# Query and key projections as seven half products, with three rotating weight slots

## The chip, the cores and the metric

The kernel runs on one core of one Trainium2 chip. The metric is the device time of one launch in microseconds (us). Engines are named as in the profile: PE (TensorE) multiplies matrices, PEld is its weight load, DVE (VectorE) and ACT (ScalarE) do elementwise work and empty PSUM, POOL is GpSimd, SP issues nearly all loads from HBM.

## The reference, cut to what matters

One inference step of a two-layer trunk on 384 tokens (128 context tokens and 256 latent tokens), width 1024, all in float32. Layer 0 is differential attention, layer 1 retention; each is followed by a mixture of 16 experts. What the change touches are the projections of queries and keys:

```python
def diff_attention(h, w_qkv, ...):
    qkv = h @ w_qkv
    q = qkv[..., :DA_QK_WIDTH].reshape(B, N, DA_HEADS, 2, DA_HEAD_DIM)        # 8 heads of 128 columns
    k = qkv[..., DA_QK_WIDTH:2 * DA_QK_WIDTH].reshape(B, N, DA_HEADS, 2, DA_HEAD_DIM)
    ...
        q = axial_rope(q)
        keys = jnp.concatenate([cached[0], axial_rope(k)], axis=1)
    ...
def retention(h, w_qkv, ...):
    kd = RET_HEADS * RET_DK                                                    # 4 heads of 256 columns
    qkv = h @ w_qkv
    q = qkv[..., :kd].reshape(B, N, RET_HEADS, RET_DK)
    k = qkv[..., kd:2 * kd].reshape(B, N, RET_HEADS, RET_DK) * (RET_DK ** -0.5)
```

Besides these the first layers' modulation `silu(cond) @ w_ada[i] + b_ada[i]` matters, because its 24 weight pieces of 2 MB ("ada" units) are streamed during attention.

## The kernel before, in words

Activations lie feature-major: `hT` holds the normalised input as 8 tiles of 128 features by 384 tokens. Each engine has its own instruction stream, written out in program order, and the streams wait for each other on semaphores.

**PSUM.** `plan_jobs` numbers every accumulation. Job n uses bank n mod 8; `open_job` makes PE wait until job n-8 is emptied by ACT or DVE. `filled` and `emptied` are the two waits.

**Weights.** `ring` has six slots of 2 MB. `plan_units` lists all weight units in the order in which SP loads them, each with its slot and with the job after whose end the slot may be loaded anew. SP is one queue in that order: in `load` it waits for the slot's former user and issues (L569); whatever stands behind it waits too. During attention slots 0 to 3 rotate over the values' weights and the ada units, slot 4 holds the queries' weights of four heads and slot 5 the keys'. The second halves of these, units ("q", 1) and ("k", 1), follow when head 3 is done.

**Attention.** Steps s = 0 to 7, one for each head. In PE's stream a step is: transposed weights of head s-2 (`turn_a`), scores of head s-1, transposes, then queries of head s (`project("q", s)`, L771), output of head s-2 (`attend`, L873 to L876), keys of head s (L771), the rotary partner of the queries (`partner`, L833), in steps 0 and 4 the values (L808), an ada product (L673), the head norm's sum (L882), the keys' partner, an ada transpose (L680) and a second ada product. DVE does softmax maxima, weights, rotary products and norms. After step 7 a tail does the last four ada products between the last heads' work, and then comes the output projection (L937).

**Retention.** For each of four heads: queries and keys (`to_features`, 4 jobs of 8 matmuls on 384 columns), then values and two gates by seven products each (`seven_products`: one full product for token tile 0, seven of 4 matmuls on 256 columns for tiles 1 and 2 together; Winograd's form of Strassen's scheme, L786). Their operand sums are made by DVE (`weight_sums`, and `hS` once), and their results joined by DVE (`join`). Then come transposes, scores, states and outputs. Slots 0 to 3 rotate over retention's weights, slot 4 holds `hS` and the partial sums, slot 5 the weight sums.

Of the kernel before, what the change touches and what calls it, by code (L numbers as in the profile page):

```python
# [16 lines left out]
P = 128  # L17
D = 1024
KT = D // P
NP_TOK, NS_TOK = 128, 256  # L20
TOK = NP_TOK + NS_TOK
TT = TOK // P
# [31 lines left out]
RSLOT = 4  # L54
# [67 lines left out]
def plan_jobs():  # L122
# [24 lines left out]
    for s in range(HEADS):  # L147
# [24 lines left out]
    seven = lambda unit, who: [(unit + (0,), who), (unit + (1,), "act")] + [(unit + (i,), "dve") for i in range(2, 8)]  # L172
# [18 lines left out]
def plan_units():  # L191

    units = [(("ada", 0, u), ("ada", 0, u), u) for u in range(4)]
    qkv = lambda kind, g: ((kind, g), (kind, g, TT - 1) if kind == "v" else (kind, HALF * g + HALF - 1))
# [6 lines left out]
    for i, u in enumerate(turning):  # L201
# [4 lines left out]
        units.append(u + (i % 4,))  # L206
    assert len(turning) % 4 == 2
    order = ((2, 3, 0, 1, 4, 5), (4, 5, 2, 3, 0, 1))
# [15 lines left out]
    for h in range(RH):  # L224
        rest += [(("rqk", h), ("rk", h, 1)), (("rv", h), ("rv", h, 7)), (("rg", h, 0), ("rg", h, 0, 7)),
                 (("rg", h, 1), ("rg", h, 1, 7)), (("state", h), ("ro", h, TT - 1, 1))]
# [3 lines left out]
    units += [(("sums", i), ("rg", RH - 1, 1, 7), 4 + i) for i in range(2)]  # L230
# [4 lines left out]
def trunk_kernel(nc, ins, outs, scratch):  # L235
# [31 lines left out]
    with ctx:  # L267
# [81 lines left out]
        oT = sq  # L349

# [34 lines left out]
        m1, u2, u3, u5 = (sums[:, 2048 + 256 * i:2304 + 256 * i] for i in range(4))  # L385
        wT_ = ring[:, 5, :].rearrange("p (n k u) -> p n k u", n=4, k=4)
# [74 lines left out]
        hS_ready, wT_ready, joined = (sem(n) for n in ("hS_ready", "wT_ready", "joined"))  # L461
# [51 lines left out]
        def slot(name):  # L513
            return ring[:, slot_of[name], :]

# [8 lines left out]
        def _(sp):  # L524
# [46 lines left out]
            for name, _, _ in UNITS:  # L571
                if name[0] == "sums":
                    continue
                if name[0] != "moe":
# [6 lines left out]
                    if name == ("rv", 0):  # L581
# [54 lines left out]
        def _(pe):  # L636
# [137 lines left out]
            def seven_products(unit, n):  # L774
# [3 lines left out]
                to_tokens(unit + (0,), w, 0)  # L778
# [25 lines left out]
            def to_tokens(name, w, t):  # L804

                b = open_job(name)
                for kt in range(KT):
                    last = mm(b, hT[:, kt, P * t:P * t + P], w[:, kt, :], start=kt == 0, stop=kt == KT - 1)  # L808
                done(last)
# [9 lines left out]
            def project(kind, h):  # L819

                g, i = h // HALF, h % HALF
                if i == 0:
                    unit_wait(pe, (kind, g))
# [1382 lines left out]
```

## Time and profile before

| | |
|---|---|
| runs | 1444.04 us median of 3 (1442.41 to 1446.9) |
| the profiled execution | 1440.93 us, of which 1439.0 us are its span |
| PE matmuls busy | 1354.5 us (94%) |
| DVE, ACT, POOL busy | 517.8, 282.2, 47.2 us |
| HBM traffic | 344.83 MB, mean 240 GB/s |
| mean granted TensorE clock | 0.983 |

The profile page shows PE busy nearly throughout. In its row of 40 slices the DMA share is high in the first quarter (attention), at nine tenths or more through the experts, and low in retention. Each float32 matmul of the program stands as two instructions in the trace, so 256 query and key matmuls are the 512 of L771. A group in a timeline covers its instructions from the first's start to the last's end; ends of PE instructions are modelled and overlap the next, so the pitch of a group is (length minus the duration of one) over (count minus one), or the distance between starts of successive groups.

### The profile page before, as it was taken

How to read it: one execution, taken by the hardware profiler on the slowest of the kernel's cores; microseconds unless marked ns; L12 is line 12 of the kernel's file. 1: busy time of each engine (PE TensorE's matmuls, PEld its weight loads, DVE VectorE, ACT ScalarE, POOL GpSimd, SP SyncE). 2: the span in 40 equal slices, each digit the busy share in tenths (PEclk: the TensorE clock that was granted, in tenths of full speed). 3: DMA queues.
4: the chain of work that ended last, by engine and by line, in shares of the span. 5: the costliest groups of instructions: out<-in, count | busy, mean ns of one | idle time of the engine just before them, and what ended most of it. 6: DMA issues, size and time to landing. Idle time of an engine off the chain costs nothing.

```text
span 1439.0 us, 17852 instructions
## 1 busy us (share of the span) xinstructions
PE 1354.5 (94%) x6816; PEld 768.3 (53%) x6816; DVE 517.8 (36%) x1376; ACT 282.2 (20%) x580; POOL 47.2 (3%) x63
## 2 busy tenths in 40 slices
PE   5899999997998999889999999999998998899997
PEld 2456556555444444447667567576565544444434
DVE  3145355625111111554464653744513311111123
ACT  3143344411010111231120221212111100001013
POOL 1001200000000000100000000100100000000010
PEclk9999999998999999999999999999999899999998
DMA  9967686926999999912323423224534799579891
GB/s 363 322 244 231 224 279 237 380 95 238 392 396 350 398 395 378 388 64 94 117 82 117 146 88 110 95 89 139 182 118 174 254 398 387 190 258 398 324 399 52
DMA packets 162742, 344.83 MB, mean 240 GB/s; under 512 B 5929, under 2 KB 23554, under 8 KB 162626
## 3 DMA queue, kind: packets, MB, share of 16 engines
q1 hardware_dynamic: 150320, 319.19, 60.4%
q10 hardware_dynamic: 9362, 14.37, 2.7%
q0 software_dynamic: 2944, 9.65, 2.5%
q8 instruction: 82, 1.34, 0.4%
q14 instruction: 34, 0.28, 0.1%
HBM read 324.96 MB, written 18.22 MB: 238 GB/s over the span
## 4 chain that ended last, share of the span: by engine, by line
PE 85%; DMA 6%; DVE 4%; ACT 2%; SPq 2%; issue 1%; DVEq 0%; ACTq 0%
PE psum L1089 14%; PE psum L771 11%; PE psum L786 10%; PE psum L808 9%; PE psum L1120 7%; PE psum L986 7%; PE psum L1206 5%; PE psum L937 3%; PE psum L1198 3%; DMA ring<-in_moe_w_up 3%; PE psum L673 2%; PE psum L1031 2%; DMA ring<-in_da_w_qkv 2%; SPq L569 1%; PE psum L1060 1%
## 5 line engine op out<-in xcount | busy, mean ns | idle before, releaser
L771 PE MATMUL psum<-hT,ring 128*128 128x384 f32 x512 | 173.5, 498 | 8.8 <-DMA ring<-in_da_w_qkv 5.9
L1089 PE MATMUL psum<-ring,work 128*64 128x512 f32 x384 | 170.1, 593 | 2.6 <-DMA ring<-in_moe_w_up 2.6
L1090 PE MATMUL psum<-ring,work 128*64 128x512 f32 x384 | 170.2, 594 | 0.0
L771 PEld LDWEIGHTS psum<-hT,ring 128*128 128x128 f32 x512 | 99.0, 195 | 77.4 <-issue 8.3
L808 PE MATMUL psum<-ring,hT 128*128 128x512 f32 x288 | 125.9, 593 | 0.0
L986 PE MATMUL psum<-work 128*128 128x128 f32 x768 | 106.4, 292 | 5.5 <-issue 3.5
L1089 PEld LDWEIGHTS psum<-ring,work 128*64 128x64 f32 x384 | 51.8, 137 | 111.2 <-issue 111.0
L986 PEld LDWEIGHTS psum<-work 128*128 128x128 f32 x768 | 95.0, 200 | 28.2 <-issue 24.0
L1120 PE MATMUL psum<-ring,work 128*64 128x512 f32 x192 | 89.9, 612 | 1.3 <-issue 1.2
L1975 DVE COPY work<-psum 128x512 f32<-128x512 f32 x32 | 22.1, 692 | 191.2 <-PE psum L1121 191.2
L1121 PE MATMUL psum<-ring,work 128*64 128x512 f32 x192 | 90.0, 613 | 0.0
L1969 DVE TENSOR_TENSOR work<-work,psum 64x512 f32<-64x512 f32 x32 | 22.1, 690 | 187.1 <-ACT work L1463 187.0
L808 PEld LDWEIGHTS psum<-ring,hT 128*128 128x128 f32 x288 | 54.8, 190 | 63.7 <-issue 62.1
L786 PE MATMUL psum<-ring 128*128 128x256 f32 x384 | 86.8, 379 | 0.0
L1463 ACT ACTIVATE work<-psum 64x512 f32<-64x512 f32 x32 | 18.8, 588 | 314.8 <-PE psum L1090 314.8
L786 PEld LDWEIGHTS psum<-ring 128*128 128x128 f32 x384 | 73.1, 190 | 9.8
L786 PE MATMUL psum<-ring,hT 128*128 128x256 f32 x288 | 66.1, 379 | 0.0
L2003 DVE TENSOR_TENSOR ring<-ring 128x1024 f32<-128x1024 f32 x48 | 60.8, 1283 | 2.5 <-DVE work L2012 1.3
L786 PEld LDWEIGHTS psum<-ring,hT 128*128 128x128 f32 x288 | 54.8, 190 | 12.5 <-issue 5.7
L1640 DVE SCALAR_TENSOR_TENSOR xT<-psum,mod,xT 128x128 f32<-128x128 f32 x70 | 24.7, 412 | 94.7 <-PE psum L1206 62.1
L1090 PEld LDWEIGHTS psum<-ring,work 128*64 128x64 f32 x384 | 51.9, 137 | 0.0
L1120 PEld LDWEIGHTS psum<-ring,work 128*64 128x64 f32 x192 | 24.9, 140 | 47.2 <-issue 45.0
(338 smaller groups left out, 1810.0 us busy)
## 6 DMA issues: line engine op xcount, KB each, us to landing
ring<-in_w_ada SPq DMA_DIRECT2D x24, 2048.0 KB, 12.4
ring<-in_moe_w_gate SPq DMA_DIRECT2D x24, 2048.0 KB, 13.0
ring<-in_moe_w_up SPq DMA_DIRECT2D x24, 2048.0 KB, 17.4
ring<-in_moe_w_down SPq DMA_DIRECT2D x24, 2048.0 KB, 17.9
ring<-in_da_w_qkv SPq DMA_DIRECT2D x6, 2048.0 KB, 14.8
sq<-in_moe_w_gate SPq DMA_DIRECT2D x8, 1536.0 KB, 12.3
hT<-in_moe_w_up SPq DMA_DIRECT2D x8, 1536.0 KB, 15.0
work<-in_moe_w_down SPq DMA_DIRECT2D x24, 512.0 KB, 11.3
```

The costliest lines, as they stand in the source:

```text
L771: last = mm(b[:, 0:TOK], w[:, kt, col:col + P], hT[:, kt, :], start=kt == 0, stop=kt == KT - 1)
L786: last = mm(b[:, 0:256], rows[k], weights[k], start=k == 0, stop=k == 3)
L808: last = mm(b, hT[:, kt, P * t:P * t + P], w[:, kt, :], start=kt == 0, stop=kt == KT - 1)
L937: last = mm(b[:, 0:TOK], w[:, h, P * (ft % 4):P * (ft % 4) + P], oT[:, h, :], start=h == 0, stop=h == HEADS - 1)
L986: last = mm(out, htok[:, t, P * kt:P * kt + P], sel[:, t].rearrange("p x s -> p (x s)"), start=t == 0, stop=t == TT - 1)
L1089: mm(psum[0:BLK, x, :], xk, wg[kt], start=kt == 0, stop=kt == KT - 1)
L1090: last = mm(psum[BLK:P, x, :], xk, wu[kt], start=kt == 0, stop=kt == KT - 1)
L1120: mm(psum[0:BLK, 5 + x, :], eaT[:, x, k, :], wd[k][:, 0:512], start=k == 0, stop=k == 3)
L1121: last = mm(psum[BLK:P, 5 + x, :], eaT[:, x, k, :], wd[k][:, 512:D], start=k == 0, stop=k == 3)
L1198: last = mm(b, a, v, start=n == 0, stop=n == len(terms) - 1)
L1206: last = mm(b[:, 0:TOK], w[:, k, P * (ft % 2):P * (ft % 2) + P], roT(k), start=k == rows[0], stop=k == rows[-1])
L2003: V.tensor_tensor(wT_[:, part], x, y, ALU.subtract).then_inc(wT_ready, 1)
```

## The change

A head's queries and keys in attention become one product with the weights as two row halves (queries, keys), the features as two halves (K), and the tokens as two halves of 192. It is computed by seven products of 4 matmuls on 192 columns instead of two jobs of 8 on 384. Retention's queries get the same (their two feature tiles are the two halves), and its keys too. Sums of operands are made by DVE in place or in freed slots; ACT keeps product 1; DVE adds up the others. In retention the values now stand before queries and keys. Slot 3 holds `hA` and partial sums during attention, slot 0 holds `fS` during retention, so three slots rotate (`RSLOT = 3`).

```diff
-RSLOT = 4
+RSLOT = 3
+QK_ORDER = (1, 2, 4, 5, 6, 3, 7)
@@ plan_jobs, attention step s
-        jobs.append((("q", s), "act"))
+        jobs += [(("qk", s, 1), "act")] + [(("qk", s, i), "dve") for i in QK_ORDER[1:]]
         if s >= 2:
             jobs.append((("o", s - 2), "dve"))
-        jobs += [(("k", s), "act"), (("qswap", s), "dve")]
+        jobs.append((("qswap", s), "dve"))
@@ plan_jobs, retention head h
-        jobs += [(("rq", h, t), "act") for t in range(2)] + [(("rk", h, t), "act") for t in range(2)]
-        jobs += seven(("rv", h), "dve") + seven(("rg", h, 0), "act") + seven(("rg", h, 1), "act")
+        jobs += seven(("rv", h), "dve") + seven(("rq", h), None) + seven(("rk", h), None)
+        jobs += seven(("rg", h, 0), "act") + seven(("rg", h, 1), "act")
@@ plan_units
-    qkv = lambda kind, g: ((kind, g), (kind, g, TT - 1) if kind == "v" else (kind, HALF * g + HALF - 1))
+    qkv = lambda kind, g: ((kind, g), (kind, g, TT - 1) if kind == "v" else ("qk", HALF * g + HALF - 1, 7))
...
-        units.append(u + (i % 4,))
+        units.append(u + (i % 3,))
...
-    order = ((2, 3, 0, 1, 4, 5), (4, 5, 2, 3, 0, 1))
+    units.append((("sums", "a"), ("qk", HEADS - 1, 7), 3))
+    order = ((3, 1, 2, 0, 4, 5), (4, 5, 0, 3, 1, 2))
@@ SP: the retention tables move behind one more unit
-                    if name == ("rv", 0):
+                    if name == ("rg", 0, 0):
@@ PE, attention
+            def project(h):
+                a11, a12, a21, a22 = qk_blocks(h)
+                if h % HALF == 0:
+                    unit_wait(pe, ("q", h // HALF))
+                    unit_wait(pe, ("k", h // HALF))
...
+                product(1, a11, hT[:, 0:4, 0:192])
+                product(2, a12, h21)
+                if h == 0:
+                    pe.wait_ge(hA_ready, 4)
+                pe.wait_ge(qkS_ready, 4 * h + 2)
+                product(4, a21, hA[:, 2])
+                product(5, qkS1, hA[:, 0])
+                product(6, a22, hA[:, 3])
+                pe.wait_ge(qkS_ready, 4 * h + 4)
+                product(3, a11, hA[:, 1])
+                product(7, a12, h22)
...
             def partner(kind, h):
-                emptied(pe, (kind, h))
+                emptied(pe, ("qk", h, 7))
@@ DVE, attention
+            def low_sums(h):
...
+                V.tensor_tensor(qkS1, a21, a22, ALU.add).then_inc(qkS_ready, 1)
+                V.tensor_tensor(a21, a11, a21, ALU.subtract).then_inc(qkS_ready, 1)
+                dve.wait_ge(qkS_ready, 4 * h + 1)
+                filled(dve, ("qk", h, 1))
+                V.tensor_tensor(a11, qkS1, a11, ALU.subtract).then_inc(qkS_ready, 1)
+                dve.wait_ge(qkS_ready, 4 * h + 3)
+                filled(dve, ("qk", h, 2))
+                V.tensor_tensor(a12, a12, a11, ALU.subtract).then_inc(qkS_ready, 1)
+            def join_qk(h):
...
+                add(raw[:, 0, 0:192], 2, am1).then_inc(evac["dve"], 1)
+                link(add(au2, 3, am1))
+                link(add(au3, 4, au2))
+                dve.sem_inc(evac["dve"], 1)
+                link(add(au5, 5, au2))
+                add(raw[:, 1, 192:TOK], 5, au3).then_inc(evac["dve"], 1)
+                add(raw[:, 1, 0:192], 6, au3).then_inc(evac["dve"], 1)
+                add(raw[:, 0, 192:TOK], 7, au5).then_inc(evac["dve"], 2)
...
                     ada([ADA_UNITS[2 * s - 1]])
+                low_sums(s)
+                if s:
                     weights_of(s - 1)
+                join_qk(s)
@@ PE, retention (seven_features has the same seven products, on 192 columns)
                 seven_products(("rv", h), 3 * h)
+                unit_wait(pe, ("rqk", h))
+                seven_features("rq", h)
+                seven_features("rk", h)
@@ DVE, retention
+                join(("rv", h), rv)
+                feature_sums("rk", h)
+                join_features("rq", h, rq)
+                rotate(0, rq)
+                weight_sums(("rg", h, 0), range(4))
+                join_features("rk", h, rk)
+                rotate(1, rk)
...
                     if h + 1 < RH:
-                        weight_sums(("rv", h + 1), ((0,), (1,), (2, 3))[t])
+                        if t < 2:
+                            weight_sums(("rv", h + 1), ((0, 1), (2, 3))[t])
+                        else:
+                            feature_sums("rq", h + 1)
```

Before the loops DVE makes `hA` (attention, 4 differences of 768 columns) and `hF` (retention, 3 of 768 and 2 of 384).

PE's stream where step 3 ends and step 4 begins, before. L673 are ada products, L771 the queries, `slot_fullN` the wait for the weights in slot N:

```order
L673 MATMUL psum<-ring,cond 32x512 [waits act_evacuated,slot_full3]
...
L673 MATMUL psum<-ring,cond 32x512 [waits act_evacuated,slot_full0]
...
L771 MATMUL psum<-hT,ring 128x384 [waits act_evacuated,slot_full4]
...
L771 MATMUL psum<-hT,ring 128x384 [waits act_evacuated,slot_full5]
...
L808 MATMUL psum<-ring,hT 128x512 [waits act_evacuated,slot_full1]
...
L673 MATMUL psum<-ring,cond 32x512 [waits act_evacuated,slot_full2]
```

The same place after; L692 are the ada products, L882 the seven products, L858 the values:

```order
L692 MATMUL psum<-ring,cond 32x512 [waits dve_evacuated,slot_full1]
...
L692 MATMUL psum<-ring,cond 32x512 [waits dve_evacuated,slot_full2]
...
L882 MATMUL psum<-hT,ring 128x192 [waits act_evacuated,slot_full5,slot_full4]
...
L858 MATMUL psum<-ring,hT 128x512 [waits dve_evacuated,slot_full0]
...
L692 MATMUL psum<-ring,cond 32x512 [waits dve_evacuated,slot_full1]
```

The first product now waits for slots 4 and 5 together. Step 4's first ada unit lies in slot 1, which step 3's first ada product still reads; before, its slot 2 had been free since step 2. In SP's list this unit stands directly ahead of ("q", 1) and ("k", 1), before and after.

DVE's stream in a step after the change, from the softmax maxima (L1717) on. L1745 to L1752 are the sums of weights, L1726 begins the softmax weights, and the adds of the products (L1759) follow these:

```order
L1717 TENSOR_REDUCE work<-psum 128x1 [waits ps_filled] x6
L1647 TENSOR_REDUCE mod<-psum 128x8 [waits ps_filled]
L1650 TENSOR_TENSOR mod<-mod,cols0 128x8 [waits dve_evacuated]
L1745 TENSOR_TENSOR work<-ring 128x512
L1746 TENSOR_TENSOR ring<-ring 128x4x128
L1749 TENSOR_TENSOR ring<-work,ring 128x4x128 [waits ps_filled,qkS_ready]
L1752 TENSOR_TENSOR ring<-ring 128x4x128 [waits ps_filled,qkS_ready]
L1726 RECIPROCAL work<-work 128x2 [waits act_evacuated]
L1727 TENSOR_TENSOR work<-work,lam_s 128x1 [waits dve_chain]
```

Before, the reciprocal stood directly behind the two rows that read and write `mod`; four sums of 512 columns now stand between.

## Rows read from the trace of the kernel before

**Rows 1.** The page: DVE's busy tenths in 40 slices; groups with busy us, mean ns.

```profile
DVE  3145355625111111554464653744513311111123
...
L771 PE MATMUL psum<-hT,ring 128*128 128x384 f32 x512 | 173.5, 498 | 8.8 <-DMA ring<-in_da_w_qkv 5.9
...
L786 PE MATMUL psum<-ring 128*128 128x256 f32 x384 | 86.8, 379 | 0.0
...
L786 PEld LDWEIGHTS psum<-ring 128*128 128x128 f32 x384 | 73.1, 190 | 9.8
```

**Rows 2.** PE's timeline of attention step 5: start us, length us, what, count.

```profile
194.80 5.33 PE L771 MATMUL psum<-hT,ring 128*128 128x384 f32 x16
...
201.49 5.32 PE L771 MATMUL psum<-hT,ring 128*128 128x384 f32 x16
...
207.17 1.92 PE L673 MATMUL psum<-ring,cond 128*32 128x512 f32 x16
209.02 0.91 PE L882 MATMUL psum<-rdiag,ones 128*128 128x384 f32 x2
...
210.21 0.60 PE L680 MATMUL psum<-base_sb,ada_rows 128*128 128x128 f32 x4
...
217.02 5.33 PE L771 MATMUL psum<-hT,ring 128*128 128x384 f32 x16
```

**Rows 3.** PE's timeline in retention, heads 0 and 2.

```profile
618.26 22.34 PE L771 MATMUL psum<-hT,ring 128*128 128x384 f32 x64 [1.85 <-DVE hT L1625]
640.44 7.03 PE L808 MATMUL psum<-ring,hT 128*128 128x512 f32 x16
...
650.76 5.34 PE L786 MATMUL psum<-ring 128*128 128x256 f32 x24
...
815.25 20.80 PE L771 MATMUL psum<-hT,ring 128*128 128x384 f32 x64
```

**Rows 4.** SP's timeline of loads: start us, length of issuing, what, count.

```profile
135.12 7.05 SPq L569 DMA_DIRECT2D ring<-in_da_w_qkv  x2
...
244.60 7.04 SPq L569 DMA_DIRECT2D ring<-in_da_w_o  x2
253.60 3.93 SPq L569 DMA_DIRECT2D ring<-in_w_ada  x2
```

**Rows 5.** DMA issues of 136 to 143 us and 256 to 258 us: KB, us to landing.

```profile
ring<-in_da_w_qkv SPq DMA_DIRECT2D x1, 2048.0 KB, 7.7
...
ring<-in_w_ada SPq DMA_DIRECT2D x1, 2048.0 KB, 14.5
```

**Rows 6.** PE's timeline at the start; a bracket is idle time and its releaser.

```profile
36.61 7.12 PE L771 MATMUL psum<-hT,ring 128*128 128x384 f32 x16 [2.56 <-DMA ring<-in_da_w_qkv]
...
47.03 7.12 PE L771 MATMUL psum<-hT,ring 128*128 128x384 f32 x16 [3.30 <-DMA ring<-in_da_w_qkv]
...
54.42 20.76 PE L808 MATMUL psum<-ring,hT 128*128 128x512 f32 x48
```

**Rows 7.** Stretches after that idle time: PE, PEld, DVE, ACT, POOL, PEclk, DMA.

```profile
48.00:51.00 3.00, 3.00 (x6) 1.49 (x6) 0.00 (x0) 0.00 (x0) 0.00 (x0) 0.50 1.05 387
51.00:54.00 3.00, 3.00 (x11) 1.81 (x10) 0.00 (x0) 0.00 (x0) 0.00 (x0) 0.97 1.05 387
```

**Rows 8.** PE's timeline at attention's end.

```profile
268.26 1.92 PE L673 MATMUL psum<-ring,cond 128*32 128x512 f32 x16
...
271.74 1.92 PE L673 MATMUL psum<-ring,cond 128*32 128x512 f32 x16 [0.20 <-DMA ring<-in_w_ada]
...
276.05 4.68 PE L937 MATMUL psum<-sq,ring 128*128 128x384 f32 x14
```

**Rows 9.** DVE's timeline in retention: sums, the end of head 1, an add.

```profile
629.89 0.69 DVE L2040 TENSOR_TENSOR ring<-hT,ring 128x512 f32<-128x512 f32 x1
...
832.93 0.69 DVE L2110 TENSOR_TENSOR work<-work 128x512 f32<-128x512 f32 x1
...
851.93 0.42 DVE L2012 TENSOR_TENSOR work<-psum,ring 128x256 f32<-128x256 f32 x1
```

More of the change, by code:

```diff
@@ L229, in plan_units @@
     turn_in()
-    units += [(("sums", i), ("rg", RH - 1, 1, 7), 4 + i) for i in range(2)]
+    units += [(("sums", i), ("rg", RH - 1, 1, 7), s) for i, s in enumerate((4, 5, 0))]
     moe(1)
@@ L349, in trunk_kernel @@
         oT = sq
+        att_end = sum(ap.shape[1] for name, ap in wa.items() if name != "at")
+        qkS1 = work[:, att_end:att_end + 512].rearrange("p (k t) -> p k t", k=4)
+        hA = ring[:, 3, 0:3072].rearrange("p (n k t) -> p n k t", n=4, k=4)
+        am1, au2, au3, au5 = (ring[:, 3, 3072 + 192 * i:3264 + 192 * i] for i in range(4))
         wr_ = carve({"tab": ret_np.shape[1], "dist": (dist_np.shape[1] + 1) // 2, "q": 2 * TOK, "k": 2 * TOK,
@@ L514, in slot, with qk_blocks @@
             return ring[:, slot_of[name], :]
+        def qk_blocks(h):
+            at = P * (h % HALF)
+            views = [slot((kind, h // HALF)).rearrange("p (k n) -> p k n", k=KT)[:, :, at:at + P] for kind in "qk"]
+            return [w[:, 4 * k:4 * k + 4, :] for w in views for k in range(2)]
         def y_rows(i):
@@ L817, in _, with product @@
             swap = table(att_tab, att_at, "swap")
[L819 to L823, printed above, removed]
-                w = slot((kind, g)).rearrange("p (k n) -> p k n", k=KT)
-                to_features((kind, h), w, P * i, 0 if (kind, h) == ("q", 0) else None)
+            def project(h):
[3 more added lines that the diff above has]
+                    unit_wait(pe, ("k", h // HALF))
+                def product(i, weights, rows):
+                    b = open_job(("qk", h, i))
+                    for k in range(4):
+                        if h == 0 and i < 3:
+                            h_wait(pe, 0, k + 4 * (i - 1))
+                        last = mm(b[:, 0:192], weights[:, k, :], rows[:, k, :], start=k == 0, stop=k == 3)
+                    done(last)
+                h21, h22 = hT[:, 4:8, 0:192], hT[:, 4:8, 192:TOK]
+                product(1, a11, hT[:, 0:4, 0:192])
[9 more added lines that the diff above has]
+                product(7, a12, h22)
             def partner(kind, h):
-                emptied(pe, (kind, h))
+                emptied(pe, ("qk", h, 7))
                 if h == 0:
@@ L1140, in _ @@
             for h in range(RH):
-                unit_wait(pe, ("rqk", h))
-                w = slot(("rqk", h)).rearrange("p (k n) -> p k n", k=KT)
-                for t in range(2):
-                    to_features(("rq", h, t), w, P * t, 2 if h == 0 and t == 0 else None)
-                for t in range(2):
-                    to_features(("rk", h, t), w, RDK + P * t)
                 def turn_o(hh, tiles=range(TT)):
@@ L1500, in _, with keep_first @@
             for h in range(RH):
[L1501 to L1508 removed]
+                def keep_first(unit, n, width=256, scale=1.0):
+                    if n:
+                        act.wait_ge(joined, n)
+                    filled(act, unit + (1,))
+                    A(m1[:, 0:width], bank(unit + (1,))[:, 0:width], ACT.Copy, scale=scale).then_inc(evac["act"], 1)
+                keep_first(("rv", h), 5 * h)
+                keep_first(("rq", h), 5 * h + 1, 192)
+                keep_first(("rk", h), 5 * h + 2, 192, RDK ** -0.5)
                 dt_ = lambda n: table(dist_tab, dist_at, n)
@@ L1517, in _ @@
                     act.wait_ge(ro_ready, TT * h)
[L1519 to L1526 removed]
                 for d in range(2):
[L1528 removed]
+                    n = 5 * h + 3 + d
                     filled(act, ("rg", h, d, 0))
```

156 lines of the change are left out of this document (115 added, 41 removed).

## The prediction

> **What bounds the kernel now.** I read four views in this order. The page first: PE works nearly throughout, so the end is set by PE's program order, and a change is worth what it takes out of that order minus the gaps it opens. Then PE's timeline of an attention step [rows 2]: the step repeats every 22.22 us (194.80 to 217.02) and its groups follow each other without a bracket of idle time, so a step lasts as long as PE's instructions. Retention is the same [rows 3]. Then SP's timeline [rows 4], because the change takes one of four rotating slots away: how early a load may start matters now. Last the start and the end of attention [rows 6, 8], the only places of that stage where PE already waits for a load: 2.56 and 3.30 us for queries' and keys' weights, 0.20 us for the last ada unit. These two places have no slack.
>
> **The gain on PE.** 384 columns cost 0.3225 us an instruction (20.80 less 0.50, over 63 [rows 1, 3]), 256 columns 0.2157 (5.34 less 0.38, over 23 [rows 1, 3]). The difference is 0.107 us for 128 columns, so 192 columns should cost 0.2157 - 0.0534 = 0.1625 us. No row shows 192 columns. From below it is 0.16 (192 columns at that slope alone). From above it is 0.19, if the weight load, which is recorded with 190 ns [rows 1], no longer hid. The nearest row is the transposes, which load 128x128 weights for only 128 columns: 4 in 0.60 us, less about 0.27 for the last one, is 0.11 us each [rows 2]. A load thus fits behind 128 columns, and I take 0.1625. The Trainium skill, "TensorE: Matmul & The Clock Gate", section "Back-to-back issue gap", says otherwise: the simple per-column formula undercounts small matmuls, which it gives as about 81 ns against 56 at 128 columns, because the weight load shares the budget. The trace's transposes do not agree with that surcharge; by it, as an estimate, the 25 ns on each of 896 instructions would take 22 us back.
>
> - Attention, a head: 32 x 0.3225 = 10.32 us becomes 7 x 4 x 2 = 56 x 0.1625 = 9.10. Gain 1.22, eight heads 9.8 us.
> - Retention, a head: 64 x 0.3225 = 20.64 becomes 112 x 0.1625 = 18.20. Gain 2.44, four heads 9.8 us.
>
> Together 19.5 us.
>
> **Start of attention.** Before, head 0's queries ran from 36.61 while the keys' weights came, and the keys began at 47.03 [rows 6]. The first product now waits for both slots, so PE stands still until 47.03 (the loads ahead of it are unchanged). Each resumption after such a gap costs: 16 instructions took 7.12 instead of 5.33 us [rows 2, 6], with the granted clock at 0.50, the 1.2 GHz level, from 48 to 51 us and 0.97 after it [rows 7]. That is 1.8 us. Products end at 47.03 + 9.10 + 1.8 = 57.9. Then the rotary partner waits for the adds: product 3 comes sixth of seven, and six adds of 192 columns hang on it, at about 0.36 us each (256 columns take 0.42 [rows 9]), 2.2 us and 0.3 of handover, against 1.3 us of product 7. 1.2 us stay open. With the partner's 0.4 us the values begin at 59.6 instead of 54.42. Lost 5.2 us, so 6.4 against the gain already counted.
>
> **The other steps.** Step 1 has the same open 1.2 us. From step 2 on `attend` (about 1.5 us between queries and keys [rows 2]) stands there and covers it. The weight sums on DVE (4 of 512 columns, 0.69 each [rows 9]) stand ahead of the softmax weights, for which ACT's third pair of exponentials waits, and with it the banks that products 6 and 3 need. Counting that chain through, it is late by about 0.2 us a step and 0.4 in step 1. The other DVE work (some 5 us a head) lies in its idle half: the slices of attention show 1 to 6 tenths [rows 1]. Cost 1.6 + 6 x 0.2 = 2.8 us; bounds 0 and 9 us (1.3 us in each of seven steps, a whole product late).
>
> **Step 4, the lost slot.** Before, ("q", 1) was issued at 135.12, right behind head 3's queries, and ("k", 1) at about 141.8 [rows 4], landing 7.7 us later [rows 5], just ahead of step 4. Now the ada unit ahead of them in SP's list reuses the slot that step 3's first ada product reads. SP stands there until that product ends: 14.22 us into the step before (194.80 to 209.02 [rows 2]), 13.2 now (1.22 less, 0.2 more). Only then three units of 2 MB go out. The first lands after 7.7 us; each further one takes 5.4 to 6.0 (the second output unit, issued at about 251.3 [rows 4], and two ada units behind it had landed 14.5 us after 257.2 [rows 5], three units in 20.4 us with 2.3 of fixed delay). The keys' weights land 19.2 us after the issue, 32.4 into step 3. PE is there at 22.22 - 1.22 + 0.2 = 21.2. It waits 11.2 us and resumes slowly for another 1.8: 13.0 us.
>
> **The tail.** The same happens in step 7. Before, the two output units and then the last two ada units were issued between 244.6 and 257.2 [rows 4]. Now ("ada", 1, 9) needs the slot of step 7's first ada product, and both output units stand behind it in the queue. From the end of that product (before: step 7 began one step after step 6, 217.02 + 22.22 = 239.24, and 14.22 on is 253.5 [rows 2]) five units follow each other: the fourth lands after about 24 us, the fifth after 7.7 + 4 x 5.6 = 30. PE wanted them 14.8 and 18.3 us after that point (268.26 and 271.74 [rows 8]). Of the 11.7 us most is spent ahead of the fourth. With half a microsecond of slow clock 12.2 us. The experts' loads behind them are late by the same amount as PE, so nothing is given back.
>
> **Retention's seams.** Head 0: DVE finishes `hS` at 630.6 [rows 9]; product 3 of the values is wanted at 618.26 + 6.9 + 3.4 + about 1.5 of slow clock = 630.1, since the queries no longer stand ahead. With handover 0.6 us. Heads 1 to 3: DVE ends the previous head at 833.6 [rows 9], now about 834.1 with `feature_sums` in place of two weight sums, and must then empty the values' first bank (0.69), which the queries' first product wants at 815.25 + 18.95 = 834.2 [rows 3]. 0.5 us a head. Together 2.1 us, bounds 0 and 8. Retention's slots are loaded at least 30 us before use even with three, at no cost; if that cover went, each would show as a DMA wait. Moving the tables behind one more unit costs nothing, since values now come first.
>
> **Sum.** 19.5 gained; 6.4 + 2.8 + 13.0 + 12.2 + 2.1 = 36.5 lost: 17 us slower. Against the profiled execution's 1440.93 that is 1458; it ran 3.1 below the median of the runs, so I put 17 on 1444.04: 1461.
>
> **Rivals.**
> - *Both waits are hidden* (SP's loads arrive in time, by faster landing or because PE is later there than I count). For it: before, both places ran with almost no wait. Against it: the semaphore waits follow from the slots, and 2 MB at the 387 GB/s of [rows 7] is 5.4 us whatever the order. Then 25.2 us fall away: 8 faster, 1436.
> - *One of them is hidden*, or both are half as long: 1449.
> - *The weight load shows at 192 columns.* At 0.19 us, 896 x 0.0275 = 24.6 us more: 1486. Against it: the transposes' 0.11 us [rows 2]. The skill's page named above would have it so.
> - *DVE becomes late in every step* (adds or bank waits at their bounds, 6 us in attention and 6 in retention above my terms): 1473. For it: these seams are the tightest part of my count.
>
> **How the numbers follow.** My case 0.65 (1452 to 1470), both hidden 0.07, one hidden 0.12, weight load 0.04, DVE late 0.12. The range 1449 to 1473 leaves the extremes out. About 0.3%, 4.3 us, is what a measurement of this kernel can tell from no change: faster 0.07, same 0.04 (from the lower end of the one-hidden case), slower 0.89.
>
> **What would show it.** In the profile after: matmuls of 192 columns at 0.16 us pitch, 896 of them; a PE wait of about 11 us for a load of `in_da_w_qkv` in attention's middle, with a clock near one half right after it; waits for `in_w_ada` of 9 and 2 us at its end; PE's start of the values near 59.6; a plain step of 21.2 us. I am wrong if step 4 begins without a DMA wait, if a plain step is not shorter than 22.2, or if retention's head is not about 2 us shorter than before.

## The result, and the profile after

The changed kernel takes 1484.11 us (median of 4 runs, 1482.38 to 1486.42) against 1445.24 (4 runs): 1.028 times, 95% interval 1.0261 to 1.0299. The forecast was 1461, with a range from 1449 to 1473. The sign was right, and so were the four costs named in attention (its start, the other steps, step 4, the tail); the size was not. One of the prediction's own signs of being wrong came true: retention's heads did not become about 2 us shorter. The profiled execution took 1482.38 us, its span 1480.6, which is 41.6 more than the span before (forecast 17, so 24.6 are missing).

The page of the changed kernel. The second, third and fourth rows are busy tenths in 40 slices and PE's granted clock; the last is PE's new product line (busy us, mean ns, idle time):

```profile
span 1480.6 us, 18884 instructions
...
PE   5799699698989999889999999999999898889997
...
DVE  2348538624211111268386484683611411111123
...
PEclk9899899898989999989999999999999899999998
...
L882 PE MATMUL psum<-hT,ring 128*128 128x192 f32 x192 | 38.4, 355 | 23.4 <-issue 12.1
```

PE's timeline of attention: the start, step 4, a plain step (5 to 6), and the end (start us, length us, what, count, idle time ahead and its releaser).

```profile
46.66 5.46 PE L882 MATMUL psum<-hT,ring 128*128 128x192 f32 x16 [10.23 <-DMA ring<-in_da_w_qkv]
...
60.42 14.75 PE L858 MATMUL psum<-ring,hT 128*128 128x512 f32 x34
...
168.70 4.50 PE L882 MATMUL psum<-hT,ring 128*128 128x192 f32 x16 [12.11 <-issue]
...
212.29 2.77 PE L882 MATMUL psum<-hT,ring 128*128 128x192 f32 x16
...
233.56 2.77 PE L882 MATMUL psum<-hT,ring 128*128 128x192 f32 x16
...
294.08 3.64 PE L692 MATMUL psum<-ring,cond 128*32 128x512 f32 x16 [11.13 <-DMA ring<-in_w_ada]
...
303.81 4.68 PE L1007 MATMUL psum<-sq,ring 128*128 128x384 f32 x14
```

The values start at 60.42 us [rows 6: 54.42], the plain step lasts 21.27 [rows 2: 22.22], step 4 waits 12.11, the tail 11.13, and the output projection begins at 303.81 [rows 8: 276.05]. The pitch at 192 columns is (2.77 - 0.355) / 15 = 0.161 us. This is the picture that was forecast, but for the tail, where one wait of 11.13 stands in place of two of 9 and 2. PE's row at step 4 names no releaser ("issue"). DVE's first weight sum waits for the same two slots; it starts at the same 168.70 and is released by the load:

```profile
168.70 0.69 DVE L1745 TENSOR_TENSOR work<-ring 128x512 f32<-128x512 f32 x1 [11.76 <-DMA ring<-in_da_w_qkv]
```

The span as a ledger of stages, from the starts of PE's groups:

| stage | before | after | more | forecast |
|---|---|---|---|---|
| to the output projection | 276.05 | 303.81 | +27.8 | +24.7 |
| to the first expert's product | 71.89 | 72.56 | +0.7 | 0 |
| experts of layer 0 | 270.32 | 281.24 | **+10.9** | 0 |
| retention, to its output projection | 393.75 | 392.57 | **-1.2** | -7.7 |
| to layer 1's first expert | 114.40 | 115.26 | +0.9 | 0 |
| experts of layer 1, to the end | 312.59 | 315.16 | +2.6 | 0 |

Two rows hold 17.4 us of the miss. Retention's -1.2 compares two single traces. The changed kernel's retention code takes 392.4 to 394.8 us in five traces (after, experiments 4, 5, 6 and 9), before's code 393.7 to 395.4 in four (before, experiments 1, 2 and 10), so a gain of about 1 us is what can be said.

In the experts nothing had been changed but the order of their slots. There the distance between the first products of neighbouring experts is the thing to read. It is 13.91 us in both kernels (24.23 where an overflow block runs, a conditional piece of code for tokens beyond an expert's first 64). Before, it exceeds that by about one microsecond at the seventh (25.17), the tenth (15.02) and, by a weight load, the fifteenth expert. After, the third takes 19.14, the fourth 19.00 and the fourteenth 18.65, 15.1 us more together. Before's own excess is gone there: the seventh takes 24.23, the tenth 13.91 and the fifteenth 12.94 (before 14.85), which leaves about 11. PE's waits in that stage, before and after (us in total, times, longest):

```profile
PE psum L1103 <- DVE work L1969: 3.8, 2, 2.3
...
PE psum L1089 <- DMA ring<-in_moe_w_up: 1.7, 1, 1.7
...
PE psum L986 <- issue: 1.0, 1, 1.0
```

```profile
PE psum L1056 <- issue: 5.2, 2, 3.4
PE psum L1190 <- issue: 3.8, 2, 3.4
PE psum L1173 <- DVE work L2073: 3.8, 2, 2.3
```

The new ones end with "issue": nothing that the profile shows released them. PE's timeline at the third and fourth experts of the changed kernel:

```profile
411.21 1.38 PE L1056 MATMUL psum<-work 128*128 128x128 f32 x10
414.40 2.07 PE L1056 MATMUL psum<-work 128*128 128x128 f32 x8 [1.81 <-issue]
...
418.60 1.12 PE L1190 MATMUL psum<-work 128*64 128x512 f32 x1
...
421.66 0.59 PE L1190 MATMUL psum<-work 128*64 128x512 f32 x1
...
432.55 0.46 PE L1173 MATMUL psum<-base_sb,work 64*128 64x64 f32 x4
...
437.23 0.61 PE L1190 MATMUL psum<-ring,work 128*64 128x512 f32 x1 [3.35 <-issue]
```

The first gap stands inside one run of 18 equal matmuls, where the program has no wait of any kind, so it is not a late load and not another engine. Behind the gap the matmuls take 1.12 instead of 0.59 us, and the rows of those stretches (PE, PEld, DVE, ACT, POOL, granted clock, DMA) have the clock at 0.52, the 1.2 GHz level, for 7 us. So a gap of 1.8 us costs 5.2 here.

```profile
414.40:421.50 7.10, 7.10 (x26) 4.56 (x28) 0.00 (x0) 0.98 (x2) 0.00 (x0) 0.52 1.03 401
421.50:430.00 8.50, 8.50 (x42) 2.67 (x38) 0.95 (x2) 0.00 (x0) 0.00 (x0) 1.00 1.05 392
```

The second gap is ACT's: PE waits for the turned activations, and ACT's timeline shows it with nothing to wait for either.

```profile
430.46 0.59 ACT L1527 ACTIVATE work<-psum 64x512 f32<-64x512 f32 x1 [11.16 <-PE psum L1160]
436.74 0.38 ACT L1530 ACTIVATE work<-psum 128x256 f32<-128x256 f32 x1 [5.69 <-issue]
```

PE's transposes that L1530 reads (L1173) ended at 433.0, so ACT stood still for 3.7 us. What lies between ACT's two instructions is a branch over the overflow block (each expert has one, on PE, ACT and DVE). The DMA records show packets of code (queues of kind "instruction") near both gaps. The queues of the stretch 411.5 to 414.0 us, and of 434.0 to 436.5 (packets, MB, share of 16 engines):

```profile
q1 hardware_dynamic: 468, 0.95, 102.1%
q8 instruction: 1, 0.02, 2.8%
```

```profile
q1 hardware_dynamic: 280, 1.02, 102.6%
q14 instruction: 1, 0.01, 0.8%
```

Packets are 16 KB in q8 and 8 KB in q14 (the page has 85 packets and 1.39 MB, 37 and 0.30), beside weight loads that fill the DMA engines. That q8 is PE's queue and q14 ACT's is inferred from these places; the profile doesn't name a queue's engine. The q14 packet stands inside ACT's gap (435.00 to 435.25, the gap 433.0 to 436.7). The q8 packet stands at 411.75 to 412.00, just ahead of PE's gap (412.59 to 414.40). A packet is no proof of a wait: layer 0's experts have 27 of q8 in either kernel, and the aligned kernel of experiment 9 has one at the same place of the third expert (7.6 us behind its first product) without a gap.

The theory from here on, called *code*: after some branches an engine waits for its own instructions, which ones depends on where the branch stands in its stretch of code, and the change shifted that by altering the length of PE's and ACT's programs. The Trainium skill, "Runtime: NRT & Kernel Launch", section "Instruction fetch mechanics", has the rule: code comes in blocks of 16 KiB, and a taken branch beyond what is held forces a fetch; the size of q8's packets agrees, while the 8 KB ones of q14 are not in the rule. The rival, called *loads*: the changed order of the experts' slots and the late start of their loads.

Retention, head 1 of the changed kernel, PE's timeline:

```profile
755.28 7.03 PE L858 MATMUL psum<-ring,hT 128*128 128x512 f32 x16
...
765.61 5.34 PE L805 MATMUL psum<-ring 128*128 128x256 f32 x24
772.86 1.97 PE L805 MATMUL psum<-ring,hT 128*128 128x256 f32 x8 [1.91 <-ACT work L1608]
774.66 1.89 PE L805 MATMUL psum<-ring 128*128 128x256 f32 x8
777.57 2.84 PE L834 MATMUL psum<-hT,ring 128*128 128x192 f32 x16 [1.02 <-DVE work L2120]
```

Two gaps where before [rows 3] had none. L1608 is ACT's head norm, which empties the bank of product 6; L2120 is DVE's copy of the first value tile, which empties the bank of the queries' first product. DVE's timeline ahead of them:

```profile
761.18 3.43 DVE L2107 TENSOR_TENSOR ring<-ring 128x1024 f32<-128x1024 f32 x2
...
771.80 0.69 DVE L2142 TENSOR_TENSOR ring<-ring 128x512 f32<-128x512 f32 x1
...
773.01 1.76 DVE L2145 TENSOR_TENSOR ring<-ring 128x512 f32<-128x512 f32 x1
774.80 0.69 DVE L2147 TENSOR_TENSOR ring<-ring 128x512 f32<-128x512 f32 x1
...
776.74 0.68 DVE L2120 COPY work<-psum 128x512 f32<-128x512 f32 x1
```

Two value sums (3.43 us, where one of 1.23 stood before) come ahead of the last tile's statistics, for which ACT waits; four query sums (3.7 us) come ahead of the copy. Heads 1 to 3 take 99.35, 97.67 and 97.88 us, before 98.4 each.

### The profile page after: what moved, and what is told of

It is laid out like the page before. It is cut to its first block, busy times and chain, and to the rows that moved or that the text cites. A ratio compares the mean times of both kernels' runs of the same rounds, so it can differ in the third digit from the quotient of the medians.

```text
span 1480.6 us, 18884 instructions
## 1 busy us (share of the span) xinstructions
PE 1351.4 (91%) x7200; PEld 826.6 (56%) x7200; DVE 599.7 (41%) x1561; ACT 271.6 (18%) x564; POOL 47.4 (3%) x63
## 3 DMA queue, kind: packets, MB, share of 16 engines
q8 instruction: 85, 1.39, 0.4%
## 4 chain that ended last, share of the span: by engine, by line
PE 77%; DVE 9%; DMA 6%; issue 3%; ACT 3%; SPq 2%; DVEq 0%; ACTq 0%
PE psum L1159 15%; PE psum L1190 8%; PE psum L805 7%; PE psum L858 7%; PE psum L1056 7%; PE psum L882 5%; PE psum L834 5%; PE psum L1272 5%; PE psum L1007 3%; DMA ring<-in_da_w_qkv 2%; PE psum L692 2%; PE psum L1101 2%; DMA out_new_ret_fwd<-work 2%; DMA ring<-in_w_ada 1%; SPq L588 1%
## 5 line engine op out<-in xcount | busy, mean ns | idle before, releaser
L858 PE MATMUL psum<-ring,hT 128*128 128x512 f32 x288 | 128.9, 604 | 1.9 <-DVE hT L1682 1.9
L858 PEld LDWEIGHTS psum<-ring,hT 128*128 128x128 f32 x288 | 55.6, 194 | 68.8 <-issue 68.5
L1697 DVE SCALAR_TENSOR_TENSOR xT<-psum,mod,xT 128x128 f32<-128x128 f32 x70 | 24.7, 412 | 94.6 <-PE psum L1272 62.1
L692 PE MATMUL psum<-ring,cond 128*32 128x512 f32 x384 | 49.1, 633 | 15.0 <-DMA ring<-in_w_ada 14.9
L882 PE MATMUL psum<-hT,ring 128*128 128x192 f32 x192 | 38.4, 355 | 23.4 <-issue 12.1
## 6 DMA issues: line engine op xcount, KB each, us to landing
work<-in_moe_w_down SPq DMA_DIRECT2D x24, 512.0 KB, 11.6
```

The costliest lines, as they stand in the source:

```text
L692: last = mm(b[32 * j:32 * j + 32, :], cond[:, kt, :], w[:, kt, :], start=kt < 4, stop=kt >= 4)
L882: last = mm(b[:, 0:192], weights[:, k, :], rows[:, k, :], start=k == 0, stop=k == 3)
```

## Experiments

A ratio is against the kernel before, run beside the experiment, with its 95% interval. An experiment of one run is read by its trace and not by its time.

**1. The slot alone.** The kernel before, with three rotating slots in attention.

```diff
-        units.append(u + (i % 4,))
-    order = ((2, 3, 0, 1, 4, 5), (4, 5, 2, 3, 0, 1))
+        units.append(u + (i % 3,))
+    order = ((3, 1, 2, 0, 4, 5), (4, 5, 3, 1, 2, 0))
```

> The kernel before with only the slot given up: three rotating slots in attention, and the experts' loads in the changed kernel's order of slots; all products as before, so every engine's code is that of before. Theory code (the experts' extra 11 us in the changed kernel are waits of PE and ACT for their own code, after the branch that each expert has): the code is the same, so the stage from the first expert's product to retention's first stays at 270.3 us, within 2. Theory loads (they come from the changed order of the experts' slots and from loads that start late): it grows to about 281 us. Both: step 4's queries wait some 11 us and cost 13 with the clock, the last two ada products wait 11 to 12, so that the output projection starts some 25 us later than before's 276.05, and the time is about 1466 us by the first theory, 1477 by the second.

1467.26 us, ratio 1.0182 (1.0152 to 1.0212). The output projection starts at 298.85, 22.8 later than before; the experts of layer 0 take 267.7 us, 2.6 less than before (expected was no change, within 2).

```profile
157.98 1.65 PE L771 MATMUL psum<-hT,ring 128*128 128x384 f32 x2 [6.58 <-DMA ring<-in_da_w_qkv]
```

```profile
287.56 3.22 PE L673 MATMUL psum<-ring,cond 128*32 128x512 f32 x16 [10.19 <-DMA ring<-in_w_ada]
...
294.54 1.92 PE L673 MATMUL psum<-ring,cond 128*32 128x512 f32 x16 [2.41 <-DMA ring<-in_w_ada]
```

The slot is worth 23 us by itself, at the two places forecast. Step 4 waits only 6.6 here (expected 11), since the queries run while the keys' weights come. The order of layer 0's slots is the changed kernel's, the stage starts 23 us late (there 28), and no time is lost in the experts: against *loads*.

**2. Attention's part alone**, retention as before with four slots (the diff's parts on `qk`, `low_sums`, `join_qk`, `project` and the three slots).

> Attention's seven half products and its three slots, retention as before with four slots. Both theories: output projection starts at 303.8 us as in the changed kernel, retention takes 394 us as before. Theory code: PE's code ahead of the experts is that of the changed kernel, so the experts of layer 0 lose the same 11 us (waits at the third, fourth and fourteenth expert), those of layer 1 something else, since the code between differs: 1480 us within 5. Theory loads: experts of layer 0 also 281 us. The two differ only in layer 1, where code gives a new pattern.

1478.25 us, ratio 1.0243 (1.0216 to 1.027). Output projection at 305.57. Layer 0's third, fourth and fourteenth experts take 19.13, 19.12 and 20.07 us; layer 1 loses less (302.3 us from its first product to PE's last instruction, after 306.9). As *code* has it, though it doesn't separate the theories in layer 0.

**3. Retention's part alone**, attention as before with four slots (the parts on `seven_features`, `feature_sums`, `join_features`, and three slots in retention).

> Attention as before with four slots, retention's queries and keys by seven half products, three slots there. Output projection at 276.05 us and experts of layer 0 at 270.3 us by both theories (code ahead of them is before's). Retention from its first product to the rows of its output projection: 392.6 us as in the changed kernel, 1.2 less than before. Theory seams (two new waits of 0.9 and 1.0 us per head from the second on take what the product saves): those waits are there again. Rival (the saving is lost only because the stage starts late in the changed kernel): the waits are gone and the stage takes 388 us. Time 1440 us by the first, 1435 by the second, and up to 5 more or less by what layer 1's experts wait for their code.

1445.82 us, ratio 1.0028 (1.0013 to 1.0043): not faster. Retention takes 394.9 us, where the first two kernels, with before's code, take 395.3 and before's own profile 393.8. Both waits are there (4.8 for ACT and 3.1 for the copy over three heads), so it is the stage's own order that eats the gain, not its late start. Layer 0's experts: 270.6 us, before's pattern. In layer 1, whose code is shifted, the second expert takes 19.00.

**4. Filler on PE.** The changed kernel with idle increments.

```diff
+            for _ in range(128):
+                pe.sem_inc(filler, 1)
```

> The changed kernel with 128 increments of a semaphore that nobody waits for, put on PE ahead of the first query product, where PE idles for 10 us. Theory code: the branches and the ends of the code's blocks stand elsewhere against each other, so the excess over 13.91 us (24.23 with an overflow block) moves to other experts; the stage's length changes by several us, up or down. Theory loads: the same experts (third, fourth, fourteenth) lose the same 5.2, 5.1 and 4.7 us, and the stage takes 281.2 us again.

1484.98 us (one run). The third and fourteenth experts are clean (13.94 and 13.91). The fourth keeps its loss (20.22: ACT's, whose code is untouched), and the tenth now takes 17.60, the thirteenth 15.06. The stage's sum stayed (280.97), where several us up or down were expected. The places moved, as only *code* has it. The filler wasn't free: step 0 begins 7.1 us later.

**5. Step 4's weights first.**

```diff
-        if u[0] == ("ada",) + ADA_UNITS[9]:
+        if u[0] == ("ada",) + ADA_UNITS[8]:
             units += [qkv("q", 1) + (4,), qkv("k", 1) + (5,)]
```

> The changed kernel with the loads of step 4's queries and keys put one place earlier in the one queue of loads, ahead of the ada unit that waits for a product of step 3. If step 4's wait of 12.1 us comes from the lost slot through that order: the loads are issued some 4 us earlier and have no 5.4 us load ahead of them, so the wait falls to about 3 us, the slow clock behind it (1.8 us) goes, and the output projection starts at about 293 us instead of 303.8. If the wait is bound by the slots of the queries themselves, it stays above 8 us. The experts' waits for code stand at the third, fourth and fourteenth expert as in the changed kernel, since PE's code is the same.

1476.18 us (one run). The wait falls from 12.11 to 2.74, and the output projection starts at 293.47, both as expected. The second is in part luck: the slow clock, which was to go, stayed (16 products took 4.50 us even behind a gap of 2.7), and 1.4 us were won at the start of attention instead, in the same code. The third expert has the gap of the changed kernel, but the clock stayed high behind it:

```profile
404.13 1.16 PE L1056 MATMUL psum<-work 128*128 128x128 f32 x8 [1.80 <-issue]
```

The granted clock of 403.5 to 411 us is 1.00, and the expert takes 15.97 instead of 19.14.

**6. The tail's slots.** Slots 3 and 4 for the last two ada units, ahead of the output projection's (the order of the experts' slots changes with them).

```diff
+        if u[0] == ("ada",) + ADA_UNITS[18]:
+            units.append((("sums", "a"), ("qk", HEADS - 1, 7), 3))
+        units.append(u + ((3, 4)[i - 20] if i >= 20 else i % 3,))
+    units += [(("wo", n), ("wo", 4 * n + 3), (5, 0)[n]) for n in range(2)]
```

> The changed kernel with the last two ada units in slots 3 and 4, which the last queries and keys leave free, and loaded ahead of the output projection's two units, which go to slots 5 and 0. If the tail's wait of 11.1 us is the order of loads and slots: it falls under 2 us and the output projection starts at about 291.5 us instead of 303.8. If the tail is bound by the transfers as such (six loads of 5.4 us one behind another), the start moves by under 4 us. Experts as in the changed kernel.

1468.51 us (one run). The wait falls from 11.13 to 2.64 and the output projection starts at 295.19, 8.6 earlier (forecast 12; the wait was to fall under 2). Most of the tail's loss was order; that the remaining 2.64 us are the transfers' was not tested.

**7. Sums early**, in retention's head norm.

```diff
-                            weight_sums(("rv", h + 1), ((0, 1), (2, 3))[t])
+                            weight_sums(("rv", h + 1), ((0, 1, 2), (3,))[t])
```

> The changed kernel with the next head's four value sums on DVE split as three and one over the first two tiles of the head norm instead of two and two. If the wait for ACT (2.6 us over three heads) comes from the two sums (3.4 us) ahead of the last tile's norm: it goes, since three sums (3.7 us) fit the first tile's gap behind the state's stores, and the second tile has one (1.2 us). The other wait (DVE's copy of the first value tile, 3.1 us) falls too, as DVE is 2.2 us earlier there. Retention's stage 392.6 us becomes 388 to 390. Rival (ACT is late by the stores of the state, not by DVE): no change.

1480.61 us (one run). The waits in heads 1 to 3, after and here:

```profile
PE psum L834 <- DVE work L2120: 3.1, 3, 1.0
PE psum L805 <- ACT work L1608: 2.6, 3, 1.9
```

```profile
PE psum L834 <- DVE work L2120: 3.1, 3, 1.0
PE psum L805 <- ACT work L1608: 1.4, 1, 1.4
```

Half a hit: the stage takes 391.5 us, not 388 to 390. Heads 2 and 3 lose ACT's wait and take 97.47, but head 1 keeps 1.4 us of it. The copy's wait did not move, but DVE did not come earlier either: its query sums begin at 771.78 us here and at 771.80 in the changed kernel, 0.2 to 0.5 us earlier in each head instead of 2.2, since what the shorter list saves goes into DVE's own waits for ACT (0.38 us idle and 1.30 instead of 0.68 for the product behind them). So this run doesn't say whether an earlier DVE would help the copy; experiment 11 moves the sums themselves.

**8. All repairs.** 5 to 7 together (slots adapted), and the values ahead of the queries and keys at steps 0 and 4, so that their weights land beside the value products; at step 4 DVE's sums go behind the softmax weights.

```diff
-    units += [qkv("q", 0) + (4,), qkv("k", 0) + (5,)]
-    turning = [qkv("v", 0)]
+    units += [qkv("v", 0) + (4,), qkv("q", 0) + (5,), qkv("k", 0) + (0,)]
+    turning = []
...
+                for g, t in value_tiles(s):
...
                 project(s)
                 if s >= 2:
                     attend(s - 2)
                 partner("q", s)
-                for g, t in value_tiles(s):
...
```

> The changed kernel with all of these, and attention's values ahead of the queries and keys at steps 0 and 4 (their unit loaded first at the start, in slot 4), so that the loads of queries and keys land beside 20.7 us of value products. Start: values from about 37 us, first ada product of step 0 at about 69 instead of 81. Step 4: no wait. Tail: none. Retention 4 us shorter. Sum 12 + 13 + 12 + 4 = 41 us off the changed kernel's 1484, about 1443, level with before; the wait for code in the experts can move it by 8 us either way. Rival (transfers bound attention as a whole): the waits come back at other loads and it stays over 1460.

1441.47 us (10 runs), ratio 0.9987 (0.9973 to 1.0). The output projection starts at 269.12, 34.7 earlier than in the changed kernel and 6.9 earlier than before. Step 4 waits for nothing; the tail, where no wait was expected, keeps 2.58 and 0.97 us, and retention is 2.6 shorter instead of 4. The third, fourth and fourteenth experts still cost 16.09, 19.18 and 17.14 though the loads are elsewhere: against *loads*.

**9. The code aligned.** The changed kernel with idle increments inside code that is jumped over.

```diff
+                        for _ in range((112, 120)[l] if e == 0 else 0):
+                            pe.sem_inc(filler, 1)
                         wd = unit(e, 2)
```

(and 15 and 6 on ACT, ahead of layer 0's and layer 1's experts; these do run, where ACT is idle).

> The changed kernel, with idle increments only: 112 (layer 0) and 120 (layer 1) in PE's code of the first expert's overflow block, which is jumped over, and 15 and 6 on ACT in idle stretches, so that from the second expert on each branch stands at the same place of its 256-instruction stretch of code (one packet of the instruction queue is 16 KB) as in the kernel before. Theory code: the waits at the third, fourth and fourteenth expert go; layer 0's stage takes 270 to 272 us instead of 281.2, and only the seventh and tenth expert have about 1 us each, as before has; layer 1 shows before's pattern too (one of 4.4 us). Time about 1474 us. Theory loads: nothing moves, 1484.

1472.47 us (4 runs), ratio 1.021 (1.0177 to 1.0242), 11.6 under the changed kernel. Layer 0's experts are 10.5 us shorter and layer 1's 2.7. The experts of layer 0 take 270.71 us: third 13.91, fourth 13.91, fourteenth 13.91, seventh 25.17, tenth 15.32, which is before's pattern. With the loads and their order those of the changed kernel, *loads* is out. PE's waits there:

```profile
PE psum L1176 <- DVE work L2080: 3.8, 2, 2.3
...
PE psum L1057 <- issue: 1.5, 2, 1.3
...
PE psum L1193 <- issue: 0.9, 1, 0.9
```

**10. Before, shifted.** The opposite: 144 and 136 increments in the kernel before, at the same place of PE's code.

> The kernel before, with 144 and 136 idle increments in the same jumped-over code of PE, so that its branches from the second expert on stand where the changed kernel has them; ACT's code is left alone. Theory code: PE's waits appear at the third expert (2 to 5 us) and the fourteenth (4 to 6 us), the fourth's (ACT's) does not; the stage takes 276 to 280 us instead of 270.3 and the kernel about 1450 us. Theory loads: 270.3 and 1443.

1448.12 us (10 runs), ratio 1.0037 (1.0017 to 1.0058). The third expert takes 15.94, the fourteenth 19.26, the fourth, which is ACT's, 13.91:

```profile
388.48 1.16 PE L987 MATMUL psum<-work 128*128 128x128 f32 x8 [1.76 <-issue]
...
565.02 3.31 PE L987 MATMUL psum<-work 128*128 128x128 f32 x14 [3.69 <-issue]
```

In layer 1 the fourth and the fifteenth take 16.54 and 16.36, as in the changed kernel. Layer 0's stage takes 273.66 us; the expected 276 was too much, since before's own waits at the seventh and tenth (2 us) vanish. So idle code that never runs slows the kernel before at the changed kernel's places.

**11. The copy first.** All repairs, and the query sums behind the copy.

```diff
                     V.tensor_copy(to[:, 0, :], bank(unit + (0,))).then_inc(evac["dve"], 1)
+                    if unit[1]:
+                        feature_sums("rq", unit[1])
```

> The kernel of all repairs, with the next head's four query sums (3.8 us on DVE) behind DVE's copy of the first value tile instead of ahead of it. If these sums are what PE waits for at retention's first query product (1.03 us, three times): the waits go and the stage falls by 3 us to 387. Rival (the copy is tied to ACT, or the sums now come late at the third query product): the wait stays or moves there, no change.

1440.03 us (one run). The copy's wait is gone in all three heads:

```profile
PE psum L805 <- ACT work L1608: 1.5, 1, 1.5
```

Heads 2 and 3 take 96.2 us, retention 386.95, 3 less than in experiment 8 and 5.6 less than in the changed kernel.

**12. All repairs, aligned.** Experiments 11 and 9 together.

> The kernel of all repairs with the sums behind the copy and the idle increments of the aligned kernel. By theory code 9 to 11 us less than the kernel of all repairs in layer 0 and 1 to 2 in layer 1, and 3 less in retention: 1441.5 - 14 = about 1428 us, 1 per cent under before. By theory loads only the 3 us: 1438.

1428.72 us (6 runs, 1426.68 to 1431.4), ratio 0.9906 (0.9883 to 0.993): faster than both kernels, by 1% and by 3.7%. PE's timeline at the start, where the values now stand first:

```profile
36.55 22.56 PE L859 MATMUL psum<-ring,hT 128*128 128x512 f32 x48 [2.51 <-DVE hT L1689]
58.95 2.76 PE L883 MATMUL psum<-hT,ring 128*128 128x192 f32 x16
```

Output projection at 270.53, experts of layer 0 270.55, retention 386.81.

## Why the prediction was right in sign and wrong in size

- **The gain on PE: right.** 0.161 us a product against 0.1625, plain step 21.27 against 21.2. A head of retention with neither of its two waits takes 96.20 (experiment 11), 2.18 less than before's 98.38, where 2.44 were forecast. (384 columns are (20.80 - 0.50) / 63 = 0.322 us, not 0.3225, 0.1 us in all.) No product runs slower than the column line, so the weight load stays hidden; the surcharge of the Trainium skill ("TensorE: Matmul & The Clock Gate", "Back-to-back issue gap") didn't appear.
- **Start of attention: right.** Values at 60.42 against 59.6.
- **The other steps: right.** Step 1 costs 0.35 us more than before (20.46 to 20.81; forecast 0.4), step 2 0.96 less (forecast 1.0).
- **Step 4: right.** 12.11 against 11.2, and 16 products in 4.50 instead of 2.77 (1.7 against 1.8; in experiments 6 and 9 the same products took 5.46 and 5.09). Experiments 1 and 5 show that it is the slot through SP's order.
- **The tail: right in mechanism, 1 us short.** From step 7's start to the output projection 48.99 us, before 36.80: 12.2 more, 11.2 forecast. In all attention cost 3.1 us more than forecast.
- **"The experts' loads behind them are late by the same amount as PE, so nothing is given back": the step that failed.** As a statement on loads it held (experiments 1 and 9). But the sum treated a stage whose instructions don't change as one whose time can't change. It had no term for where the code lies. PE and ACT stand still at places that depend on where their code lies, and the shift made layer 0 10.9 us dearer (experiments 4, 9 and 10), nearly half of the 24.6 us of span by which the forecast missed. That the fourth expert's wait follows ACT's code and the others PE's is shown by experiments 4 and 10, which move PE's alone; that they wait for the fetch of code is inferred from the packets. Of the 10.9, 3.1 are the clock behind the third expert's gap, and luck: the clock fell there in two of the eight traces that have the gap. No row of before was read for it, though its experts already showed two such distances (25.17 and 15.02).
- **Retention's seams: the second step that failed, by a term left out and one too small.** The term of 2.1 us became 8.6 (7.7 gained by forecast for the stage, 1.2 measured), just outside the bound of 8 that the prediction gave. ACT's wait for the head norm (2.6 us; 4.8 in experiment 3) was missing from the list: the split of the value sums into two and two was costed at nothing. DVE's copy was seen but put at 0.5 us a head and came to 1.0: one of the four sums ahead of it took 1.76 instead of 0.69 us. About 0.4 a head is not traced (the values' products last 19.36 us without the waits, before 18.95, at a granted clock of 1.00 behind both gaps), and head 0 gained 0.9 where 1.8 was forecast. Experiment 11 shows the copy's cause. Experiment 7 shows ACT's in part: head 1 waits 1.9 to 2.8 us for ACT with two sums ahead of the last tile (six traces) and 0.8 to 1.5 with one (four traces), so a rest has another cause, which was not settled.
- **Layer 1's experts, +2.6:** the same kind of waits, by their places (after, the fourth and the fifteenth expert take 16.66 and 16.26 us, before, the twelfth 18.26, which the aligned kernel has again with 17.75). **Up to the experts and behind retention, 0.7 and 0.9:** not traced.
- **The rivals.** None of them held. "DVE late in every step" had the right place in retention and the wrong one in attention.

## What to carry to other kernels

In this program, whose experts have branches, the length of the code ahead is an input of the time: a change that left the stage's instructions alone moved it by 4% of that stage. All these waits stood where weight loads filled the DMA engines; whether it takes that was not tested. So compare the distances between like pieces before and after, and don't credit or blame the edit before the code is aligned. A resource given up (here a load slot) is priced by what stands behind it in the queue: 23 us of slot for 20 us of products, most of it bought back by reordering loads and by putting work whose weights are there ahead of work whose weights are late. Where an engine waits for an item of another engine's list, shortening the list far ahead of the item can be swallowed by that engine's own waits (experiment 7); putting the item ahead of the work in front of it took the wait away (experiment 11).

## What the runs showed of the hardware

- A wait bound to the place of the code, read as a wait for instructions: 1.7 to 2.0 us inside a run of equal matmuls and 3.2 to 3.7 us on PE or ACT behind a branch, with the DMA engines at 102% share. Experiment 10 made it with instructions that never run, experiment 9 removed it with such on PE and 15 idle increments on ACT. What makes a place bad, and why the wait differs by kind, stays open.
- The first of these costs 2.1 us alone or 5.2 with the clock: the third expert took 19.14 and 19.13 us after and in experiment 2, 15.97 and 15.96 in experiments 5 and 7, for the same gap of 1.8.
- 128 semaphore increments on PE took at most 19.2 us, 0.15 us each, which is nearly a 192-column product; they are not free as filler in front of work. It is an upper bound, since PE also waits for a load there.
- The granted clock can fall behind a gap of under 2 us: it was 1.00 from 407 to 411 us, and 0.52, the 1.2 GHz level, for the 7 us behind the gap of 1.81. Behind the same gap in experiment 5 it stayed at 1.00.
